# Constant-tile matmuls in TensorE's pauses inside the layer norms, the mean subtracted two tiles ahead, and a shorter pooling body

## The reference, cut to what matters

```python
def layer_norm(x, g, b):
    mu = xf.mean(-1, keepdims=True)
    var = jnp.square(xf - mu).mean(-1, keepdims=True)
    return ((xf - mu) * lax.rsqrt(var + LN_EPS) * g + b).astype(x.dtype)
# update of a sub-layer: x <- LayerNorm(ALPHA * x + gate * sublayer(x * (1 + scale) + shift))
# pooling, per channel group with window win (2, 4, 8, 16), cs the running sum over tokens, cnt = hi - lo:
    parts.append((cs[:, hi, sl] - cs[:, lo, sl]) / cnt - hf[:, :, sl])
```

## Time and profile before

| | us |
|---|---|
| median of 3 runs | 4079.28 (4078.37 to 4088.55) |
| the profiled execution, its own time | 4078.95 |
| its span | 4077.2 |

### The profile page before, as it was taken

How to read it: one execution, slowest core, us unless ns; L and a number is a source line. 1 busy time by engine, 2 the same in 40 slices (tenths; PEclk the granted TensorE clock), 3 DMA queues, 4 the chain that set the end, 5 groups by cost and what they waited for, 6 DMA issues and landing times.

```text
span 4077.2 us, 74246 instructions
## 1 busy us (share of the span) xinstructions
PE 3614.5 (89%) x31392; PEld 3404.8 (84%) x31392; DVE 2526.7 (62%) x3537; ACT 905.6 (22%) x1764; POOL 1855.7 (46%) x881
## 2 busy tenths in 40 slices
PE   8998989999789468886999995599999989999997
PEld 3877889999678358886899995499998877889997
DVE  5366588757782166663887577888487556552125
ACT  5422220001242145542200011200012322120001
POOL 1310256656265345544566663266564310356662
PEclk9999999999899669897999998799999999999998
DMA  8100023433144244322243331134332100122221
GB/s 312 57 16 11 27 89 131 136 121 109 63 164 145 82 99 94 95 58 95 83 140 135 109 124 55 42 130 145 106 128 69 43 17 11 47 63 73 78 73 52
DMA packets 225834, 369.53 MB, mean 91 GB/s; under 512 B 104640, under 2 KB 109568, under 8 KB 225408
## 3 DMA queue, kind: packets, MB, share of 16 engines
q1 hardware_dynamic: 167840, 250.82, 19.8%
q10 hardware_dynamic: 57696, 114.21, 8.0%
HBM read 327.46 MB, written 37.52 MB: 90 GB/s over the span
## 4 chain that ended last, share of the span: by engine, by line
PE 68%; DVE 18%; ACT 4%; issue 4%; DMA 1%; ACTq 1%; POOL 1%; SPq 0%; DVEq 0%; POOLq 0%
PE ps L733 49%; DVE f_acc L1863 4%; PE ps L991 3%; PE ps L967 3%; PE ps L977 2%; PE ps L1053 1%; DVE m_mx L2089 1%; PE ps L946 1%; DVE x L1960 1%; PE ps L771 1%; DVE x L1969 1%; PE ps L927 1%; DVE x L1990 1%; PE ps L788 1%; DVE r_hlo L2140 1%
## 5 line engine op out<-in xcount | busy, mean ns | idle before, releaser
L601 POOL TENSOR_TENSOR w_hi<-w_raw,zrow 128x1024 fp32r<-128x1024 f32 x354 | 700.0, 1977 | 1836.2 <-PE ps L733 1017.4
L603 POOL TENSOR_TENSOR w_lo<-w_raw,w_hi 128x1024 fp32r<-128x1024 f32 x354 | 905.5, 2558 | 27.8
L733 PE MATMUL ps<-f_hhi,w_hi 128*128 128x320 f32 x2688 | 637.9, 319 | 13.3 <-DVE f_a L2003 12.8
L1863 DVE SCALAR_TENSOR_TENSOR f_acc<-f_unit,silu_c,f_acc 128x512 f32<-128x512 f32 x504 | 642.3, 1315 | 7.6
L733 PE MATMUL ps<-f_hhi,w_lo 128*128 128x320 f32 x2688 | 615.3, 310 | 0.0
L733 PE MATMUL ps<-f_hlo,w_hi 128*128 128x320 f32 x2688 | 612.6, 309 | 0.0
L733 PEld LDWEIGHTS ps<-f_hhi,w_hi 128*128 128x128 f32 x2688 | 442.7, 189 | 16.1 <-DVE f_a L2003 16.1
L733 PEld LDWEIGHTS ps<-f_hlo,w_hi 128*128 128x128 f32 x2688 | 451.7, 189 | 0.0
L733 PEld LDWEIGHTS ps<-f_hhi,w_lo 128*128 128x128 f32 x2688 | 451.2, 189 | 0.0
L733 PE MATMUL ps<-f_ahi,w_hi 128*128 128x320 f32 x1408 | 322.0, 310 | 0.0
L733 PE MATMUL ps<-f_ahi,w_lo 128*128 128x320 f32 x1408 | 320.8, 309 | 0.0
(11 more groups left out here) (382 smaller groups left out, 6694.8 us busy)
## 6 DMA issues: line engine op xcount, KB each, us to landing
w_raw<-in_w SPq DMA_DIRECT2D x349, 512.0 KB, 3.5
f_unit<-in_ada_w ACTq DMA_DIRECT2D x72, 1024.0 KB, 5.8
ada_ring<-in_ada_w SPq DMA_DIRECT2D x24, 1024.0 KB, 6.2
up_scratch<-r_o ACTq DMA_DIRECT2D x40, 320.0 KB, 2.3
s_LW<-up_scratch SPq DMA_DIRECT2D x16, 320.0 KB, 4.8
s_LA<-up_scratch SPq DMA_DIRECT2D x8, 640.0 KB, 6.4
x<-in_x SPq DMA_DIRECT2D x1, 2560.0 KB, 9.7
x_scratch<-r_o ACTq DMA_DIRECT2D x8, 320.0 KB, 2.2
```

What stands on the lines that cost most here:

```text
L601: nc.gpsimd.tensor_tensor(whi[:, slot, :], raw[:, raw_slot, :], zrow[:, 0:1].to_broadcast([P, CH * P]), ALU.add).then_inc(w_hi_done, 1)
L603: nc.gpsimd.tensor_tensor(wlo[:, slot, :], raw[:, raw_slot, :], whi[:, slot, :].bitcast(F32), ALU.subtract).then_inc(w_split, 1)
L733: last = mm(ps[:, 2 * b + h, 0:HT], w, r[:, h * HT:(h + 1) * HT], start=kt == 0 and n < 2, stop=kt == KT - 1 and n >= 4)
L1863: last = stt(acc[:, cd, :], unit[:, k, :], by, acc[:, cd, :], ALU.mult, ALU.add)
```

## The change

Three edits.

1. `RUN_ON = 6` fp32 matmuls of `ones` with the first 320 columns of the constants follow PE's four transposes in each norm, into pair 2, once DVE's first `total` has read that pair (a new semaphore `rd`, also waited on by DVE where the chain's wait stood). Another six, into pair 0, follow `spread` in all norms but the last. Nothing reads them. DVE's other `total`s keep their chain waits.
2. The default of `ahead` goes from 3 to 2.
3. In the pooling, ACT applies gain and bias to `x` (one instruction per tile, after its cast; DVE waits for all eight before it gates). The division by the count becomes a scaling by the constant 1/w inside the subtraction; only the columns at the ends of the two token groups are multiplied beforehand by w times the inverse count (two tiny operations for each tile of window 2, four for the others). The clearing covers only the columns that stay zero.

```diff
+RUN_ON = 6
@@ totals (PE)
                 turned(t, m.S[:, 3, :], 1)
+                pe.wait_ge(q.rd, q.at.rd + 1)
+                run_on(2)
+
+            def run_on(b):
+
+                for n in range(RUN_ON):
+                    mm(ps[:, 2 * b + n % 2, 0:HT], ones, cst[:, 0:HT], start=True, stop=True)
@@ spread (PE)
                     last.then_inc(q.bc, 1)
+                if t < 2 * DEPTH - 1:
+                    run_on(0)
@@ pooling (ACT)
                     nc.scalar.copy(m.hhi[:, kt, :], m.t32[:, kt % 2, :]).then_inc(qq.hi, 1)
+                    act.wait_ge(q.hp, kt + 1)
+                    af(x[:, kt, :], x[:, kt, :], ACT.Identity, bias=lna[:, 1, 1, kt:kt + 1],
+                       scale=lna[:, 1, 0, kt:kt + 1]).then_inc(q.xs, 1)
@@ scales (DVE)
-                total(1, 2)
-                total(2, 3)
+                total(1, 2).then_inc(q.rd, 1)
+                dve.wait_ge(q.rd, q.at.rd + 1)
+                ch(total(2, 3))
@@ normalise (DVE)
-            def normalise(t, step, ahead=3):
+            def normalise(t, step, ahead=2):
@@ pooling (DVE)
                     dve.wait_ge(q.hp, kt + 1)
-                    ts(x[:, kt, :], x[:, kt, :], lna[:, 1, 0, kt:kt + 1], lna[:, 1, 1, kt:kt + 1], ALU.mult, ALU.add)
...
-                    for t0, t1, d0 in ((0, TS, 16), (TS, T, 48)):
-                        last = tt(t32[:, t0:t1], cur[:, t0 + d0 - hw:t1 + d0 - hw], m.cnt[:, g, t0:t1], ALU.mult)
+                    SEGMENTS = ((0, TS, 16), (TS, T, 48))
+                    for t0, t1, d0 in SEGMENTS:
+                        for e0, e1 in ((t0, t0 + hw), (t1 - hw + 1, t1)):
+                            if e1 > e0:
+                                edge = cur[:, e0 + d0 - hw:e1 + d0 - hw]
+                                last = stt(edge, edge, float(w), m.cnt[:, g, e0:e1], ALU.mult, ALU.mult)
                     ch(last)
-                    for t0, t1, d0 in ((0, TS, 16), (TS, T, 48)):
-                        last = tt(t32[:, t0:t1], t32[:, t0:t1], hp[:, t0 + d0:t1 + d0], ALU.subtract)
+                    for t0, t1, d0 in SEGMENTS:
+                        last = stt(t32[:, t0:t1], cur[:, t0 + d0 - hw:t1 + d0 - hw], 1.0 / w, hp[:, t0 + d0:t1 + d0],
+                                   ALU.mult, ALU.subtract)
...
-                nc.vector.memset(m.b[:, :, :], 0.0)
-                nc.vector.memset(m.hp[:, :, :], 0.0).then_inc(q.st, 1)
+                nc.vector.memset(m.b[:, :, N - 16:N], 0.0)
+                nc.vector.memset(m.hp[:, :, 0:16], 0.0)
+                nc.vector.memset(m.hp[:, :, TS + 16:TS + 48], 0.0)
+                nc.vector.memset(m.hp[:, :, N - 16:N], 0.0).then_inc(q.st, 1)
                 dve.wait_ge(q.st, 1)
                 normalise(2 * L - 1, lagging)
                 body(KD - 1)
+                dve.wait_ge(q.xs, KD)
```

More of the change, by code:

```diff
@@ L397, in build @@
         q_split = dict(zip(splits, uses("split", dict(val=KD, hi=KD, lo=KD), len(splits))))
-        q_ln = uses("ln", dict(ksum=1, d=2, sh=KD - 2, sq=KD, cp=2, red=4, acc=2, tr=4, var=1, sd=1, diag=2, bc=2, cen=KD, nrm=KD), 2 * DEPTH)
+        q_ln = uses("ln", dict(ksum=1, d=2, sh=KD - 2, sq=KD, cp=2, red=4, acc=2, tr=4, rd=1, var=1, sd=1, diag=2, bc=2, cen=KD, nrm=KD), 2 * DEPTH)
         ln_fin = sem("ln_fin")
@@ L409, in build @@
         s_zld = [sem(f"rwb_zload{i}") for i in range(KD // 2)]
-        q_pool = sems("pool", "cst st hp")
+        q_pool = sems("pool", "cst st hp xs")
         class Ends:
@@ L1933, in total @@
                     src = ps[:, 2 * b:2 * b + 2, :].rearrange("p b c -> p (b c)")[:, 0:T].rearrange("p (j t) -> p j t", j=NCH)
-                    ch(nc.vector.tensor_reduce(cols[:, n, :], src, AX.X, ALU.add))
+                    return nc.vector.tensor_reduce(cols[:, n, :], src, AX.X, ALU.add)
                 def diagonal(n, c):
@@ L1938, in diagonal @@
                        cols[:, c, :].unsqueeze(2).to_broadcast([P, NCH, P]), ALU.mult).then_inc(q.diag, 1)
-                total(1, 2)
-                total(2, 3)
+                total(1, 2).then_inc(q.rd, 1)
+                dve.wait_ge(q.rd, q.at.rd + 1)
+                ch(total(2, 3))
                 ts(cols[:, 1, :], cols[:, 1, :], -1.0 / D, None, ALU.mult)
                 ch(ts(cols[:, 2, :], cols[:, 2, :], 1.0 / D, None, ALU.mult))
-                total(3, 0)
+                ch(total(3, 0))
                 ch(stt(cols[:, 0, :], cols[:, 3, :], -1.0 / D, cols[:, 1, :], ALU.mult, ALU.add))
-                total(4, 1)
+                ch(total(4, 1))
                 ch(tt(cols[:, 1, :], cols[:, 0, :], cols[:, 0, :], ALU.mult))
```

## The result

The median of the changed kernel is 4054.18 us (four runs, 4053.02 to 4065.66) against 4082.19 beside it: ratio 0.9936 [0.9913, 0.9959]. The forecast was 4061.5.

A forecast was written before the change was run, and what follows sets the result against it. PE was taken to bound the kernel with 68% of the chain, DVE 18%. Clocks 7.2, two ahead 2.0, clearings 2.1 and body 6.4 made 17.7 us off 4078.95 profiled, forecast as 4061.5 on the median's footing; range 4056 to 4069.

The forecast's parts named there:

- The clock in the spread, 6 x 1.06: In six norms (t = 0, 1, 3, 5, 6, 7) the spread runs at full clock, each gaining 1.06 us, 6.4 together.
- t = 4: Norm entered after 12.85 idle us: run-on delays the spread by 0.45, yet 0.35 gained; nothing if clock rises 1 us later.
- Rival 5: Run-on at half clock in the norm t = 4 alone, ending at 2614.3; 4065 us, chance 0.05.
- The run-ons' worth, 7.2: Full clock in the spreads of the norms: 6.4 for six norms, 0.5 for t = 2, 0.35 for t = 4.
- Nothing else sits behind it on PE: Step for the spread in the norms: full clock gains only DVE's shorter wait there, 1.06 us a norm.
- Rival 3: Behind norms t = 0, 2, 4 and in pooling, POOL holds up one DVE operation more (4068) or fewer (4058); chance 0.11.
- The second run-on costs and gains nothing: Run-on behind the spread: PE's next work comes 6 us after the spread in t = 0; no cost, no gain.
- Two ahead, 2.0: One centred tile fewer ahead of the first multiplication: 0.43 us in t = 0, 2, 4 and 0.34 in two norms.
- Clearings 2.1, body 6.4: Pooling of layer 2: shorter clearings ahead of the first total gain 2.1 us; the eight bodies gain 6.4.
- rival 2: Pooling: ACT becomes the bound or tiny operations cost 0.2 us each; 4 us of the body go, 4065.5, chance 0.09.
- Rivals 1 and 4: First: run-on doesn't hold the clock, spread starts at 1.2 GHz, 4069 us, chance 0.08. Second: see rival 4.
- rival 4: Run-on at half clock takes 6.4 us, delaying each norm's spread by 2.6, eight times 21; 4090 us, chance 0.03.

The follow-up runs named there:

- e12: Changed kernel plus three fp32 matmuls of constants ahead of the second product of the FFNs of layers 0 to 2; median 4044.97 us, ratio 0.9901 to before.
- e2: Kernel before with only the default of ahead taken from 3 to 2; median 4084.13 us, ratio 1.0005 to before.
- e3: Kernel before with the pooling edits alone, no run-ons and three tiles ahead; median 4075.50 us, ratio 0.9982 to before.
- e7: Changed kernel with RUN_ON = 12, twelve matmuls in each run-on in place of six; median 4079.81 us, ratio 0.9990 to before.
- e4: Changed kernel run once more, unedited; median 4058.58 us, ratio 0.9933 to before.
- e11: Kernel before plus three fp32 matmuls of constants ahead of the second product of the FFNs of layers 0 to 2; median 4065.39 us, ratio 0.9950 to before.

## Why the prediction came out as it did

*The clock in the spread, 6 x 1.06: right, 0.10 short in size.* DVE starts 1.38 behind the spread where 1.48 was forecast, 1.16 gained a norm. t = 2 gave 0.6 (0.5 forecast). All waits together gave 8.2 to 8.6 against 7.2.

*t = 4: right in the mean.* The run-on delays the spread, and the stage took 7.06 and 7.53 in two executions against 7.70 and 8.00: 0.2 to 0.9 gained, 0.35 forecast. Rival 5 would have had 6.4 us in this run-on; it took 3.40. In e12 it took 4.29 and the stage 8.29, so there nothing was gained, as the forecast had said for a clock that rises 1 us later. The rule of the Trainium skill on transposes ("TensorE: Matmul & The Clock Gate", Part 4) would have given the 6.4 of rival 5; no execution agrees with it.

*The run-ons' worth, 7.2: this is the term that was mis-sized.* Measured alone it is 18.7. The mechanism of the waits was right; missing were the 8 us of the heads behind t = 0, 2 and 4. "Nothing else sits behind it on PE" looked at the next instruction only. Rival 3 named the place, gains and sums that meet POOL differently, and gave it 3.5 us of gain at most (4058): it counted single operations of DVE that one more or one fewer split holds up. The step to be mended is that size: a shift does not move one meeting but ends or keeps a rhythm of up to six products, worth 3 to 8 us a layer.

*The second run-on costs and gains nothing:* no run shows a cost. Whether it gains stays open, at 4.5 us in medians.

*Two ahead, 2.0: not visible.* Alone it is +0.3 us with an interval that reaches 1.6 of gain, because of the 0.58 of e2, which the forecast had named as a condition ("1.07 at full clock"). Behind a run-on the first product comes 0.4 earlier, as worked out for one norm (0.43).

*Clearings 2.1, body 6.4: right.* 2.76 and 6.85 in the stage table (the latter with two tiles ahead), 8.4 by the medians of e3 against 8.5. The clearings gave more since a small one costs 0.09 where 0.17 was taken; ACT's bound showed where it was put, 0.36 and 0.35 ahead of bodies 5 and 6 and 1.09 ahead of body 7, and rival 2 did not come.

*Rivals 1 and 4:* refuted by the window at 1.00 and by the run-on of 3.4 us. e7 shows that rival 4 had the price of a late run-on right: a delay of 2.5 us a norm against its 2.6. Its 4090 us for the whole also had the spreads at half clock and nothing gained in the heads; e7 took 4079.8.

*The footing:* the profiled execution of before, on which the sum stood, was 4.9 us below the median of 23 later runs (4083.86), and its heads and RWKV layer were on the short side (916.5). That hid part of the gain in the comparison with it, and no row of one profile could have told. So it is in part luck that the forecast time lies as near as it does: the gain was forecast as 17.7 us and measured as 28.0 beside before in the first runs and as 25.3 in e4, and the short base took 3 to 5 us of that error back. The 4058.58 of e4 lies inside the range; the first median does not.

## What to carry to other kernels

Fill an engine's pause ahead of a short critical operation with work on constants if the clock falls in that pause, and make the filler shorter than the pause: six matmuls gained 1.16 us a norm, twelve lost 2.5 against them. Where two engines hold each other up and a third paces them, look at the intervals between repeated products over the whole stretch before pricing an edit that shifts its start; a product every 16.3 us where every 14.8 is possible is a gain by itself. Have the filler start as soon as the pause does: begun 2.39 us into it, it met the lower clock itself. Take more than one profile of before as the base of a sum: stages that no edit touches differed here by 12 us between executions.

## What the hardware showed unexpectedly

- Adding 1.6 us of matmuls to each of three layers made the kernel 18.8 us faster (e11), with the heads at 194.4 us instead of 198 to 202.
- The same pause of TensorE, 2.43 and 2.42 us at the same place of the same FFN, was followed by a granted clock of 1.00 in before and of 0.50 in e4, and the stretch with the fall was the shorter one, 198.0 us against 201.7.
- Eight gains on 128x640 took 11.62 us on DVE: 0.61 each for four, 2.18 to 2.70 for the four beside POOL's splits. The Trainium skill, "SBUF — State Buffer", "Who interferes with whom", has the two engines lock a shared port pair against each other; the rows agree. They add that the blocking can keep itself going for 100 us.
- A clearing of 32 columns took 0.09 us and one of 1408 columns 1.23.
